# Three reorderings in a one-core encoder kernel: the opening's copies and weight split, the conv chunks in the attention, the Ln and Exp of the head norms

## The chip, the core and the metric

The kernel runs on one core of a Trainium2 chip. The core has a matrix engine (TensorE, PE in the trace), VectorE (DVE), ScalarE (ACT), GpSimd (POOL) and a queue that only starts transfers (SyncE, SP). Each engine takes its instructions in program order; between engines there are only semaphores, so an instruction that waits holds everything behind it on its engine. The metric is the time of one execution on the device, in microseconds.

## The reference, cut to what matters

```
h = x                                                          # 512 tokens x 1024
# layer 0
hn   = rms_norm(h, norm_mix[0]);  proj = hn @ w_in             # u, q, k, v
u    = silu(layer_norm(conv31(u_a * sigmoid(u_b)) + conv_b))   # 4 chunks of 128 channels
a    = softmax(s0 + bias) - lam * softmax(s1 + bias)           # 4 heads, 2 maps each
o    = rms_norm(a @ v, subln_g) * (1 - lam_init)
h   += concat([u, o]) @ w_out
# layer 1: RWKV-7 time mixing
xr, xw, xk, xv, xa, xg = [hn + hh * mu[i] for i in range(6)]
r, k, v = xr @ w_r, xk @ w_k, xv @ w_v
kk   = k * k_k;  kk = kk / max(sqrt(sum(kk^2, per head)), 1e-12)
...                                                            # two wkv7 scans, norm, gate
# after each: cross-attention into 256 memory tokens, squared-ReLU MLP (4096 hidden); at the end rms_norm
```

All is float32. The large products are made of three passes: each operand is split into a rounded high part and a low rest, and TensorE adds hi\*hi, hi\*lo and lo\*hi.

## The kernel before

Activations lie transposed: 8 chunks of 128 channels by 512 tokens. Weights come in slots of 1024 x 256 (1 MB); three raw slots `w` are filled by SyncE in turn. Each slot is split by two instructions: `Split.round` on ScalarE writes the high part (L326) and `Split.rest` on VectorE subtracts it from the raw weights (L344). Activation chunks are split in the same way, `Pair.round` (L405) and `Pair.rest` (L410). A product of 128 output channels is 24 matmuls (L357 to L359). Four PSUM banks are used in turn for numbered jobs: TensorE takes the bank of job n when the reader of job n-4 has freed it. No scheduler runs: the order on each engine is the order in which the code is written, or a list that all engines walk through.

*Opening* (`stage_in`). TensorE transposes x chunk by chunk (jobs jx+c, L651). VectorE copies chunks 0 to 3 to `h` (L799), ScalarE chunks 4 to 7 (L716), after it has summed the squares of the rows and made the roots (L710 to L712). VectorE multiplies the identity by the roots (L802), TensorE spreads them over all partitions (L655), and `Norm.start_dve` and `start_act` make the normalised chunks (L518) and their high and low parts. The first product starts when slot 0 is split and chunk 0 has its low part, and goes on chunk by chunk. `start_act` and `start_dve` already contain calls of `ws.round(act, 0)` and `ws.rest(dve, 0)`; such a call does nothing for a slot that is done.

*Differential attention* (`Differential`). All engines walk the list `order`. For i = 0 to 15, pair i is the two maps of one head and one block of queries: ("s", i, c) are its scores, TensorE's product (L972), VectorE's bias and maximum (L1026), ScalarE's exp (L1070). ("k", ...) is half a product of layer 1's memory keys, filler for TensorE (L982, copied by ScalarE in L1079). ("d", i) is the difference of the two maps on VectorE (L1034 to L1040), ("t", i) its transpose (L990, copied in L1087), "o" the product with v (L998), "n" the sum of squares for the head norm, whose Ln and Exp are ScalarE's L1105 and L1108, "m" and "M" the scaled head output and its split. ("A", c) splits conv chunk c, which is ready before the list begins: ScalarE's L405, VectorE's L410. What it makes is used by the output projection, after the list.

*Key projection of the recurrent layer* (`rin_act`, `rin_dve`). For t = 0 to 7: VectorE mixes chunk t of xv (L1900), ScalarE rounds it (L405) and copies key chunk t out of its bank (L1800), VectorE makes the low part (L410), scales the key (L1957) and squares it (L1962). TensorE sums the squares of a head (L1759), VectorE clamps the sum at 1e-24 (L1970) at step t for chunk t-2, ScalarE makes Ln and Exp, that is the reciprocal root (L1859, L1862), VectorE multiplies (L1975). Odd steps also split a weight slot. TensorE's order is k0, k1, k2, n0, k3, n1, ... k7, n5, n6, v0, n7, v1 ...; v0 needs the low part of chunk 7.

Of the kernel before, what the change touches and what calls it, by code (L numbers as in the profile page):

```python
# [21 lines left out]
ALU = mybir.AluOpType  # L22
ACT = mybir.ActivationFunctionType
# [7 lines left out]
C = D // P  # L31
# [505 lines left out]
def stage_in(k, cat):  # L537


    i = k.i  # L540
# [163 lines left out]
    def in_act(act):  # L704
# [8 lines left out]
        ws.round(act, 0)  # L713
        for c in range(4, C):
            k.wait_full(act, jx + c)
            act.activation(k.h[:, c, :], k.bank(jx + c), ACT.Copy).then_inc(k.free(jx + c), 1)  # L716
# [21 lines left out]
        for x in seq:  # L738
            kind, n = x
# [49 lines left out]
    def in_dve(dve):  # L789
# [7 lines left out]
        for c in range(4):  # L797
            k.wait_full(dve, jx + c)
            dve.tensor_copy(k.h[:, c, :], k.bank(jx + c)).then_inc(k.free(jx + c), 1)  # L799
        dve.wait_ge(s_root, 1)  # L800
        for a in range(4):
            dve.tensor_scalar(diag[:, a, :], k.ident, xst[:, 8 + a:9 + a], None, ALU.mult).then_inc(s_diag, 1)  # L802
        ws.rest(dve, 0)
# [112 lines left out]
class Differential:  # L916
# [3 lines left out]
    def __init__(self, k, cat, first):  # L920
# [17 lines left out]
        for i in range(16):  # L938
            order += [("s", i, 0), ("s", i, 1), ("k", i // 2, i % 2)]
            if i:  # L940
                order.append(("d", i - 1, 0))
            for lag, kind in ((3, "o"), (4, "n"), (5, "m"), (6, "M")):
                if i >= lag and (i - lag) % 4 == 3:
                    order.append((kind, (i - lag) // 4, 0))
            if i >= 2:
                order.append(("t", i - 2, 0))
            if i in (1, 3, 5, 7):
                order.append(("A", i // 2, 0))
# [659 lines left out]
def stage_rwkv_in(k):  # L1608
# [4 lines left out]
    with ExitStack() as cx:  # L1613
# [158 lines left out]
        def rin_act(act, lead):  # L1772
# [71 lines left out]
            for t in range(16):  # L1844
# [9 lines left out]
                if 3 <= t < 11 and t % 2:  # L1854

                    b = t - 3
                    for n in (b, b + 1):
                        k.wait_freed(act, num[("n", n)])
                        k.act(act.activation(rn[:, n % 4, :], rn[:, n % 4, :], ACT.Ln))  # L1859
                    k.act.wait(act)  # L1860
                    for n in (b, b + 1):
                        act.activation(rn[:, n % 4, :], rn[:, n % 4, :], ACT.Exp, scale=-0.5).then_inc(s_rt, 1)  # L1862
# [23 lines left out]
        def rin_dve(dve):  # L1886
# [65 lines left out]
            for t in range(16):  # L1952
# [19 lines left out]
                if 4 <= t < 12:  # L1972
                    b = t - 4
                    dve.wait_ge(s_rt, b + 1)
                    dve.tensor_tensor(kk[:, b, :], kk[:, b, :], rn[:, b % 4, :], ALU.mult).then_inc(s_kk, 1)  # L1975
# [996 lines left out]
```

## Time and profile before

| | us |
|---|---|
| three executions | 1918.66, 1923.87, 1922.09 (median 1922.09) |
| the profiled execution | 1918.66 |
| its span | 1916.8 |
| TensorE busy | 1856.4 (97%) |
| VectorE busy | 1053.4 (55%) |
| ScalarE busy | 745.4 (39%) |

Times in the rows count from the start of the span; 1.9 us of the execution lie around it. TensorE's busy time is that of pipelined instructions whose ends are modelled, so it says that the engine is fed, not that it is at its peak. Where one engine is busy nearly all the time, the places to read are its few waits and, in front of each, the queue of the engine that it waited for.

### The profile page before, as it was taken

How to read it: one execution, taken by the hardware profiler on the slowest of the kernel's cores; microseconds unless marked ns; L12 is line 12 of the kernel's file. 1: busy time of each engine (PE TensorE's matmuls, PEld its weight loads, DVE VectorE, ACT ScalarE, POOL GpSimd, SP SyncE). 2: the span in 40 equal slices, each digit the busy share in tenths (PEclk: the TensorE clock that was granted, in tenths of full speed). 3: DMA queues.
4: the chain of work that ended last, by engine and by line, in shares of the span. 5: the costliest groups of instructions: out<-in, count | busy, mean ns of one | idle time of the engine just before them, and what ended most of it. 6: DMA issues, size and time to landing. Idle time of an engine off the chain costs nothing.

```text
span 1916.8 us, 38658 instructions
## 1 busy us (share of the span) xinstructions
PE 1856.4 (97%) x17053; PEld 1527.7 (80%) x17053; DVE 1053.4 (55%) x1404; ACT 745.4 (39%) x999; POOL 174.5 (9%) x136
## 2 busy tenths in 40 slices
PE   6999999999999999999999999999999999999997
PEld 5898668778888888775779898988777788888886
DVE  4997755444432442538659787877754444324422
ACT  4534664344321332323644333443643353213322
POOL 1000002010000001210012111111220010000000
PEclk9999999999999999999999999999999999999999
DMA  6226233212233233433441111112352122332221
GB/s 214 89 87 217 76 99 132 67 62 92 88 110 98 89 99 110 162 110 127 159 141 45 50 50 50 51 47 70 125 201 85 44 88 92 106 110 87 90 88 44
DMA packets 165503, 189.41 MB, mean 99 GB/s; under 512 B 11801, under 2 KB 152646, under 8 KB 163674
## 3 DMA queue, kind: packets, MB, share of 16 engines
q1 hardware_dynamic: 162016, 174.44, 28.7%
q0 software_dynamic: 3088, 12.45, 1.6%
q8 instruction: 135, 2.21, 0.5%
q14 instruction: 30, 0.25, 0.0%
q10 hardware_dynamic: 234, 0.06, 0.0%
HBM read 161.22 MB, written 21.51 MB: 95 GB/s over the span
## 4 chain that ended last, share of the span: by engine, by line
PE 51%; DVE 4%; issue 2%; ACT 1%; DMA 1%; ACTq 0%; DVEq 0%; SPq 0%
PE ps L357 10%; PE ps L359 10%; PE ps L358 10%; PE ps L2356 7%; PE ps L2322 2%; PE ps L2369 2%; PE ps L2310 1%; PE ps L2333 1%; PE ps L1313 1%; PE ps L1743 1%; PE ps L2415 1%; PE ps L2289 1%; PE ps L2452 1%; PE ps L1294 1%; PE ps L2381 1%
## 5 line engine op out<-in xcount | busy, mean ns | idle before, releaser
L344 DVE TENSOR_TENSOR weights_split<-w,weights_split 128x2048 fp32r<-128x2048 f32 x116 | 265.6, 2290 | 235.8 <-ACT weights_split L326 231.1
L326 ACT ACTIVATE weights_split<-w 128x2048 fp32r<-128x2048 f32 x118 | 225.5, 1911 | 290.5 <-PE ps L359 270.6
L357 PE MATMUL ps<-x_hn_hi,weights_split 128*128 128x512 f32 x640 | 252.7, 395 | 0.0
L359 PE MATMUL ps<-x_hn_hi,weights_split 128*128 128x512 f32 x640 | 249.2, 389 | 0.0
L358 PE MATMUL ps<-x_hn_lo,weights_split 128*128 128x512 f32 x640 | 249.0, 389 | 0.0
L357 PE MATMUL ps<-f_hidden_hi,weights_split 128*128 128x512 f32 x512 | 199.3, 389 | 0.0
L359 PE MATMUL ps<-f_hidden_hi,weights_split 128*128 128x512 f32 x512 | 199.2, 389 | 0.0
L358 PE MATMUL ps<-f_hidden_lo,weights_split 128*128 128x512 f32 x512 | 199.2, 389 | 0.0
L1563 DVE SCALAR_TENSOR_TENSOR f_relu<-ps,x_squares 128x512 f32<-128x512 f32 x64 | 44.1, 691 | 191.1 <-PE ps L359 172.5
L358 PEld LDWEIGHTS ps<-x_hn_lo,weights_split 128*128 128x128 f32 x640 | 120.2, 188 | 26.4 <-issue 1.4
L357 PEld LDWEIGHTS ps<-x_hn_hi,weights_split 128*128 128x128 f32 x640 | 120.2, 188 | 26.0 <-issue 1.4
L359 PEld LDWEIGHTS ps<-x_hn_hi,weights_split 128*128 128x128 f32 x640 | 120.1, 188 | 25.1
L462 POOL TENSOR_TENSOR x_squares<-x_squares 128x512 f32<-128x512 f32 x36 | 50.4, 1401 | 948.8 <-ACT x_squares L454 948.1
L1447 ACT ACTIVATE f_squared<-f_relu 128x512 f32<-128x512 f32 x64 | 40.4, 631 | 200.7 <-DVE f_relu L1563 200.7
L358 PEld LDWEIGHTS ps<-f_hidden_lo,weights_split 128*128 128x128 f32 x512 | 96.1, 188 | 20.1
L359 PEld LDWEIGHTS ps<-f_hidden_hi,weights_split 128*128 128x128 f32 x512 | 96.1, 188 | 19.9
L357 PEld LDWEIGHTS ps<-f_hidden_hi,weights_split 128*128 128x128 f32 x512 | 96.1, 188 | 19.8
L357 PE MATMUL ps<-x_src_hi,weights_split 128*128 128x512 f32 x256 | 103.8, 405 | 4.6 <-DVE weights_split L344 3.3
L359 PE MATMUL ps<-x_src_hi,weights_split 128*128 128x512 f32 x256 | 99.8, 390 | 0.0
L358 PE MATMUL ps<-x_src_lo,weights_split 128*128 128x512 f32 x256 | 99.7, 390 | 0.0
L357 PE MATMUL ps<-r_mix_hi,weights_split 128*128 128x512 f32 x192 | 78.9, 411 | 4.0 <-DVE r_mix_lo L410 2.9
L2268 POOL TENSOR_TENSOR s_levels<-s_b_scores_rows,con 128x1024 f32<-128x1024 f32 x24 | 56.4, 2363 | 277.2 <-PE ps L2381 182.7
(365 smaller groups left out, 3496.7 us busy)
## 6 DMA issues: line engine op xcount, KB each, us to landing
w<-in_ffn_w_up_dram SPq DMA_DIRECT2D x32, 1024.0 KB, 5.4
w<-in_ffn_w_down_dram SPq DMA_DIRECT2D x32, 1024.0 KB, 5.0
w<-in_xattn_w_kv_dram SPq DMA_DIRECT2D x15, 1024.0 KB, 5.4
w<-in_ab_w_in_dram SPq DMA_DIRECT2D x10, 1024.0 KB, 5.1
w<-in_xattn_w_q_dram SPq DMA_DIRECT2D x8, 1024.0 KB, 5.0
w<-in_xattn_w_o_dram SPq DMA_DIRECT2D x8, 1024.0 KB, 5.0
w<-in_ab_w_out_dram SPq DMA_DIRECT2D x4, 1024.0 KB, 5.4
w<-in_rwkv_w_r_dram SPq DMA_DIRECT2D x4, 1024.0 KB, 6.5
```

The source lines that it names most:

```text
L326: act.activation(hi, raw, ACT.Copy).then_inc(k.w_hi_ready, 1)
L344: eng.tensor_tensor(lo, raw, hi.bitcast(F32), ALU.subtract).then_inc(k.w_lo_ready, 1)
L357: pe.matmul(out, lhs[0], rhs[0], start=start, stop=False)
L358: pe.matmul(out, lhs[0], rhs[1], start=False, stop=False)
L359: return pe.matmul(out, lhs[1], rhs[0], start=False, stop=stop)
L462: pool.tensor_tensor(self.acc, former, self.sq[:, c % 2, :], ALU.add).then_inc(self.s_acc, 1)
L1447: act.activation(r2[:, n % 2, :], rl[:, n % 2, :], ACT.Square).then_inc(s_r2, 1)
L1563: dve.scalar_tensor_tensor(rl[:, n % 2, :], k.bank(up[half] + n), 0.0, rs, ALU.max, ALU.mult) \
L2268: pool.tensor_tensor(lm[:, l - 1], bb[:, p % 2, :, :, 0, :], over(k.mask(f"Z{l}"), NC, 2), ALU.mult) \
L2322: m = pe.matmul(bank(kind, p, h)[HP[z], i * P:(i + 1) * P], kb[r, u, c, z, :], ar[r, b, :, c, z, :], start=True, stop=True)
L2356: m = pe.matmul(k.ps[r, 6 + h, at(c)], lhs, rhs, start=True, stop=True)
L2369: m = pe.matmul(bank(kind, p, h)[r, i * P:(i + 1) * P], xt[r, h, c, :], ra[r, c, h, :, :].rearrange("p a t -> p (a t)"), start=True, stop= ...
```

## The change

Three places are edited, with no change of what is computed. In the opening ScalarE copies chunks 4, 6 and 7 and VectorE chunk 5 (behind the diagonals), and the first weight slot is split inside `start_act` and `start_dve`, on ScalarE after the copies and on VectorE behind two normalised chunks. In the attention the four ("A", c) entries move from the ends of iterations 1, 3, 5 and 7 to iterations 1, 2, 3 and 4, ahead of the difference. In the key projection Ln and Exp are done for one chunk at each step from t=2, instead of for two chunks at each odd step from t=3, and VectorE's multiplication comes one step earlier.

```
--- before.py
+++ after.py
@@ -710,8 +710,7 @@
             k.act.link(act, act.activation(xsq[:, :], xn[:, a, :], ACT.Square, accum_out=xst[:, a:a + 1]))
         k.act.link(act, act.activation(xst[:, 4:8], xst[:, 0:4], ACT.Ln, bias=k.eps[:, 0:1], scale=1.0 / D))
         act.activation(xst[:, 8:12], xst[:, 4:8], ACT.Exp, scale=-0.5).then_inc(s_root, 1)
-        ws.round(act, 0)
-        for c in range(4, C):
+        for c in (4, 6, 7):
             k.wait_full(act, jx + c)
             act.activation(k.h[:, c, :], k.bank(jx + c), ACT.Copy).then_inc(k.free(jx + c), 1)
         nrm.start_act(act, ws)
@@ -794,13 +793,14 @@
             n = sum(r for _, r in ROWS[g])
             k.wait_full(dve, jp + g)
             dve.tensor_copy(k.par[:, g * P:g * P + n], k.bank(jp + g)[:, 0:n]).then_inc(k.free(jp + g), 1)
-        for c in range(4):
+        for c in (0, 1, 2, 3, 5):
+            if c == 5:
+                dve.wait_ge(s_root, 1)
+                for a in range(4):
+                    dve.tensor_scalar(diag[:, a, :], k.ident, xst[:, 8 + a:9 + a], None, ALU.mult) \
+                       .then_inc(s_diag, 1)
             k.wait_full(dve, jx + c)
             dve.tensor_copy(k.h[:, c, :], k.bank(jx + c)).then_inc(k.free(jx + c), 1)
-        dve.wait_ge(s_root, 1)
-        for a in range(4):
-            dve.tensor_scalar(diag[:, a, :], k.ident, xst[:, 8 + a:9 + a], None, ALU.mult).then_inc(s_diag, 1)
-        ws.rest(dve, 0)
         dve.wait_ge(s_rs, 1)
         for n in (jp + 2, *range(jx, jx + C)):
             k.wait_freed(dve, n)
@@ -937,6 +937,8 @@
         order = []
         for i in range(16):
             order += [("s", i, 0), ("s", i, 1), ("k", i // 2, i % 2)]
+            if 1 <= i <= 4:
+                order.append(("A", i - 1, 0))
             if i:
                 order.append(("d", i - 1, 0))
             for lag, kind in ((3, "o"), (4, "n"), (5, "m"), (6, "M")):
@@ -944,8 +946,6 @@
                     order.append((kind, (i - lag) // 4, 0))
             if i >= 2:
                 order.append(("t", i - 2, 0))
-            if i in (1, 3, 5, 7):
-                order.append(("A", i // 2, 0))
         order += [("d", 15, 0), ("R", "01", "01"), ("m", 2, 0), ("t", 14, 0), ("R", "01", "23"), ("M", 2, 0),
                   ("t", 15, 0), ("R", "23", "0"), ("o", 3, 0), ("R", "23", "1"), ("n", 3, 0), ("R", "01", "456"),
                   ("R", "23", "23"), ("m", 3, 0), ("M", 3, 0), ("R", "01", "7"), ("R", "23", "4567")]
@@ -1851,15 +1851,12 @@
                     ws.round(act, t // 2 + 6)
                 if t in (12, 13):
                     lead(t - 12)
-                if 3 <= t < 11 and t % 2:
-
-                    b = t - 3
-                    for n in (b, b + 1):
-                        k.wait_freed(act, num[("n", n)])
-                        k.act(act.activation(rn[:, n % 4, :], rn[:, n % 4, :], ACT.Ln))
-                    k.act.wait(act)
-                    for n in (b, b + 1):
-                        act.activation(rn[:, n % 4, :], rn[:, n % 4, :], ACT.Exp, scale=-0.5).then_inc(s_rt, 1)
+                if 2 <= t < 10:
+
+                    b = t - 2
+                    k.wait_freed(act, num[("n", b)])
+                    k.act.link(act, act.activation(rn[:, b % 4, :], rn[:, b % 4, :], ACT.Ln))
+                    act.activation(rn[:, b % 4, :], rn[:, b % 4, :], ACT.Exp, scale=-0.5).then_inc(s_rt, 1)
 
         def rin_pool(pool):
             for c in range(C):
@@ -1969,8 +1966,8 @@
                         dve.wait_ge(s_kk, b - 3)
                     dve.tensor_scalar(rn[:, b % 4, :], k.bank(num[("n", b)]), 1e-24, None, ALU.max) \
                        .then_inc(k.free(num[("n", b)]), 1)
-                if 4 <= t < 12:
-                    b = t - 4
+                if 3 <= t < 11:
+                    b = t - 3
                     dve.wait_ge(s_rt, b + 1)
                     dve.tensor_tensor(kk[:, b, :], kk[:, b, :], rn[:, b % 4, :], ALU.mult).then_inc(s_kk, 1)
         k.scan_inputs = [(s_out[b], 16 * 8) for b in range(2)] + [(s_vout[b], 16 * 4) for b in range(2)] \
```

VectorE at the start of the program. `x_roots` are the diagonals with the roots, `in_hn_full` the normalised chunks, and the rows with `weights_split` the low part of a slot.

```order
-L799 COPY h<-ps 128x512 x4
-L802 TENSOR_SCALAR x_roots<-con,x_stats 128x128 x4
-L344 TENSOR_TENSOR weights_split<-w,weights_split 128x2048
+L795 COPY par<-ps 128x117
+L795 COPY par<-ps 128x124
+L795 COPY par<-ps 128x88
+L803 COPY h<-ps 128x512 x4
+L800 TENSOR_SCALAR x_roots<-con,x_stats 128x128 x4
+L803 COPY h<-ps 128x512
 L518 SCALAR_TENSOR_TENSOR in_hn_full<-h,par,ps 128x512 x2
+L344 TENSOR_TENSOR weights_split<-w,weights_split 128x2048
 L410 TENSOR_TENSOR in_hn_lo<-in_hn_full,in_hn_hi 128x512
```

The split of the slot moved from ahead of the two normalised chunks to behind them, and a fifth copy stands ahead. The copies of `par` are those of before with other line numbers.

VectorE in the attention, from the second score of pair 1 on; before:

```order
L1026 ISA scores,softmax_stats<-ps,bias 128x512
L1026 ISA softmax_stats 128x1
L1034 RECIPROCAL softmax_stats<-softmax_stats 128x2
L1035 TENSOR_TENSOR softmax_stats<-softmax_stats,lam 128x1
L1039 TENSOR_SCALAR difference<-scores,softmax_stats 128x512
L1040 SCALAR_TENSOR_TENSOR difference<-scores,softmax_stats,difference 128x512
```

and after:

```order
L1026 ISA scores,softmax_stats<-ps,bias 128x512
L1026 ISA softmax_stats 128x1
L410 TENSOR_TENSOR x_src_lo<-cat,x_src_hi 128x512
L1034 RECIPROCAL softmax_stats<-softmax_stats 128x2
L1035 TENSOR_TENSOR softmax_stats<-softmax_stats,lam 128x1
L1039 TENSOR_SCALAR difference<-scores,softmax_stats 128x512
L1040 SCALAR_TENSOR_TENSOR difference<-scores,softmax_stats,difference 128x512
```

The low part of conv chunk 0, which before stands behind these rows, moved ahead of the difference of pair 0. Before, the next three stand behind the differences of pairs 2, 4 and 6; after, one stands ahead of each of the differences of pairs 1, 2 and 3.

ScalarE in the key projection, from the rounding of chunk 2 of xv to the step of chunk 3. `memt` holds the clamped sums.

```order
 L405 ACTIVATE r_mix_hi<-r_mixed 128x512
 L1800 ACTIVATE r_staged<-ps 128x512
+L1858 ACT_TABLE_LOAD
+L1858 ACTIVATE memt<-memt 128x512
+L1859 ACT_TABLE_LOAD
+L1859 ACTIVATE memt<-memt 128x512
 L405 ACTIVATE r_mix_hi<-r_mixed 128x512
 L1800 ACTIVATE r_staged<-ps 128x512
 L326 ACTIVATE weights_split<-w 128x2048
+L1858 ACT_TABLE_LOAD
+L1858 ACTIVATE memt<-memt 128x512
 L1859 ACT_TABLE_LOAD
```

A load, an Ln, a load and an Exp are new behind the copy of key chunk 2, where nothing stood; the odd step that follows has one Ln and one Exp where it had two and two. In this stretch the program before has 8 table loads and the changed one 16.

## Rows read from the trace of the kernel before

**Rows 1.** The page, busy time of the engines: us, share, instructions.

```profile
PE 1856.4 (97%) x17053; PEld 1527.7 (80%) x17053; DVE 1053.4 (55%) x1404; ACT 745.4 (39%) x999; POOL 174.5 (9%) x136
```

**Rows 2.** Timeline of the opening: start, duration (us), engine, line, operation, [idle before <-releaser].

```profile
14.85 1.92 ACT L326 ACTIVATE weights_split<-w 128x2048 fp32r<-128x2048 f32 x1 [0.57 <-DMA w<-in_ab_w_in_dram]
...
16.48 1.16 PE L655 MATMUL ps<-x_roots,con 128*128 128x128 f32 x8
...
16.68 2.03 ACT L716 ACTIVATE h<-ps 128x512 f32<-128x512 f32 x4
...
16.81 2.29 DVE L344 TENSOR_TENSOR weights_split<-w,weights_split 128x2048 fp32r<-128x2048 f32 x1 [0.38 <-ACT weights_split L326]
...
19.02 1.40 DVE L518 SCALAR_TENSOR_TENSOR in_hn_full<-h,par,ps 128x512 f32<-128x512 f32 x2
...
20.45 0.69 DVE L410 TENSOR_TENSOR in_hn_lo<-in_hn_full,in_hn_hi 128x512 fp32r<-128x512 f32 x1
...
21.29 0.77 PE L357 MATMUL ps<-in_hn_hi,weights_split 128*128 128x512 f32 x1 [3.65 <-DVE in_hn_lo L410]
```

**Rows 3.** Timeline in the attention, all engines, pairs 2 to 6.

```profile
202.91 0.69 DVE L410 TENSOR_TENSOR x_src_lo<-cat,x_src_hi 128x512 fp32r<-128x512 f32 x1 [0.56 <-ACT x_src_hi L405]
...
206.42 0.69 DVE L1026 CUSTOM_DVE_ANT_0 scores<-ps,bias 128x512 f32<-128x512 f32 x1
...
207.65 0.16 DVE L1034 RECIPROCAL softmax_stats<-softmax_stats 128x2 f32<-128x2 f32 x1
...
207.88 0.71 ACT L1070 ACTIVATE scores<-scores,softmax_stats 128x512 f32<-128x512 f32 x1
...
208.12 1.13 PE L972 MATMUL ps<-keys,q 64*128 64x512 f32 x4
...
208.44 0.75 DVE L1040 SCALAR_TENSOR_TENSOR difference<-scores,softmax_stats,difference 128x512 f32<-128x512 f32 x1
...
208.59 0.36 ACT L1079 ACTIVATE mem_keys<-ps 128x256 f32<-128x256 f32 x1
...
209.32 0.62 ACT L405 ACTIVATE x_src_hi<-cat 128x512 fp32r<-128x512 f32 x1
...
210.05 0.69 DVE L410 TENSOR_TENSOR x_src_lo<-cat,x_src_hi 128x512 fp32r<-128x512 f32 x1 [0.86 <-ACT x_src_hi L405]
...
211.54 1.13 PE L972 MATMUL ps<-keys,q 64*128 64x512 f32 x4
...
217.97 3.60 PE L998 MATMUL ps<-difference_t,v 128*128 128x512 f32 x8
```

**Rows 4.** Timeline in the attention, around pairs 8 to 10.

```profile
230.09 1.12 PE L972 MATMUL ps<-keys,q 64*128 64x512 f32 x2 [0.39 <-ACT difference_t L1087]
...
230.66 0.69 DVE L410 TENSOR_TENSOR x_src_lo<-cat,x_src_hi 128x512 fp32r<-128x512 f32 x1 [4.80 <-ACT x_src_hi L405]
...
237.07 1.13 PE L972 MATMUL ps<-keys,q 64*128 64x512 f32 x4
```

**Rows 5.** Timeline of the key projection, TensorE, VectorE and ScalarE.

```profile
923.40 0.62 ACT L405 ACTIVATE r_mix_hi<-r_mixed 128x512 fp32r<-128x512 f32 x1
...
925.78 0.68 DVE L1970 TENSOR_SCALAR memt<-ps 128x512 f32<-128x512 f32 x1
...
927.76 0.63 ACT L405 ACTIVATE r_mix_hi<-r_mixed 128x512 fp32r<-128x512 f32 x1 [3.26 <-DVE r_mixed L1900]
...
936.65 0.61 ACT L405 ACTIVATE r_mix_hi<-r_mixed 128x512 fp32r<-128x512 f32 x1
...
942.46 0.47 PE L357 MATMUL ps<-r_mix_hi,weights_split 128*128 128x512 f32 x1 [1.12 <-issue]
```

**Rows 6.** ScalarE's groups, 900 to 950 us: count | busy us, mean ns | idle.

```profile
L1859 ACT ACT_TABLE_LOAD x3 | 3.8, 1283 | 0.1
```

**Rows 7.** Stretches: us, busy by engine, PEclk (granted clock), DMA share, GB/s.

```profile
21.70:24.70 3.00, 3.00 (x8) 2.35 (x8) 2.93 (x6) 1.98 (x3) 0.00 (x0) 0.51 1.04 373
...
232.90:236.20 3.30, 3.30 (x8) 2.43 (x8) 3.23 (x7) 1.63 (x5) 0.00 (x0) 0.50 0.00 0
```

More of the change, by code:

```diff
@@ L712, in in_act @@
         act.activation(xst[:, 8:12], xst[:, 4:8], ACT.Exp, scale=-0.5).then_inc(s_root, 1)
-        ws.round(act, 0)
-        for c in range(4, C):
+        for c in (4, 6, 7):
             k.wait_full(act, jx + c)
@@ L796, in in_dve @@
             dve.tensor_copy(k.par[:, g * P:g * P + n], k.bank(jp + g)[:, 0:n]).then_inc(k.free(jp + g), 1)
-        for c in range(4):
+        for c in (0, 1, 2, 3, 5):
+            if c == 5:
+                dve.wait_ge(s_root, 1)
+                for a in range(4):
+                    dve.tensor_scalar(diag[:, a, :], k.ident, xst[:, 8 + a:9 + a], None, ALU.mult) \
+                       .then_inc(s_diag, 1)
             k.wait_full(dve, jx + c)
             dve.tensor_copy(k.h[:, c, :], k.bank(jx + c)).then_inc(k.free(jx + c), 1)
[L800 to L803, printed above, removed]
         dve.wait_ge(s_rs, 1)
@@ L939, in __init__ @@
             order += [("s", i, 0), ("s", i, 1), ("k", i // 2, i % 2)]
+            if 1 <= i <= 4:
+                order.append(("A", i - 1, 0))
             if i:
@@ L946, in __init__ @@
                 order.append(("t", i - 2, 0))
-            if i in (1, 3, 5, 7):
-                order.append(("A", i // 2, 0))
         order += [("d", 15, 0), ("R", "01", "01"), ("m", 2, 0), ("t", 14, 0), ("R", "01", "23"), ("M", 2, 0),
@@ L1853, in rin_act @@
                     lead(t - 12)
[L1854 to L1862, printed above, removed]
+                if 2 <= t < 10:
+                    b = t - 2
+                    k.wait_freed(act, num[("n", b)])
+                    k.act.link(act, act.activation(rn[:, b % 4, :], rn[:, b % 4, :], ACT.Ln))
+                    act.activation(rn[:, b % 4, :], rn[:, b % 4, :], ACT.Exp, scale=-0.5).then_inc(s_rt, 1)
         def rin_pool(pool):
@@ L1971, in rin_dve @@
                        .then_inc(k.free(num[("n", b)]), 1)
-                if 4 <= t < 12:
-                    b = t - 4
+                if 3 <= t < 11:
+                    b = t - 3
                     dve.wait_ge(s_rt, b + 1)
```

## The prediction

> **What bounds the kernel now.** I read the busy times first: TensorE is busy 97% of the span [rows 1]. A saving on another engine is worth nothing unless TensorE waits for it, and each wait that TensorE gains lengthens the run. So I read, for each of the three places edited, the timeline of the three engines: when a TensorE instruction waited, for whom, and how late the engine it waited for already was. The first place is the opening, where TensorE idles 3.65 us before its first weight product [rows 2]. The second is the differential attention, where TensorE is continuously fed except around 230 us [rows 3, 4]. The third is the key projection of the recurrent layer, where its one wait, 1.12 us, ends at 942.46 [rows 5]. Behind each, TensorE is the bound again and has no slack in absolute time, so a delay at one place is carried to the end.
>
> **The opening.** VectorE's order is the path. Before, it splits the first weight slot (2.29 us from 16.81) while TensorE spreads the row roots (16.48 to 17.64) and ScalarE copies x (16.68 to 18.71); the normalised chunks start at 19.02 and the first low part at 20.45 [rows 2]. After, VectorE copies chunk 5 (0.69) behind the diagonals and then waits for the root spread, which still runs from 16.48 to 17.64, as nothing ahead of the diagonals has changed. ScalarE no longer splits at 14.85; it copies three chunks, the last as soon as TensorE has transposed it (by 16.5), to about 17.1, then splits to 19.0 (1.92). VectorE: two normalised chunks from 17.7, 1.4 us; weight split from 19.1, 2.2; first low part at 21.3 instead of 20.45. What was hidden beside the root spread now stands between it and the product. From there VectorE is busy without a break to the eighth low part, so the whole start is 0.9 us late. Bounds: 0 if the split could still hide, +2.3 if all of it (the row's 2.29) is added. I take +0.9. Loading the fourth slot starts as late as that split ends, 2.3 us later, and has some 15 us before ScalarE wants it: nothing.
>
> **The attention.** Before, TensorE repeats two scores, half a key product and a transpose every 3.42 us (208.12 to 211.54) [rows 3]. VectorE takes both scores (206.42 to 207.65), then the difference of the pair before (0.79 to the start of its last instruction, 0.75 for that), and only then the low part of a conv chunk, at 210.05, for which it waits on ScalarE's rounding [rows 3]. The difference fills most of that wait. After, the low part comes first and VectorE stands still through ScalarE's latency. From the first score: the second exp starts 1.46 us later (207.88), is done 0.71 later (208.59), rounding 0.62, handover 0.11 (209.94 to 210.05): 2.90; low part 0.61; difference 1.54 and handover 0.04: 5.1 us a pair, and 0.26 more where ScalarE copies a key product in between. Four of these: the first low part stays at 202.91 [rows 3], since ScalarE's queue ahead of it is the same; with it done (0.61) and the first difference (1.58), the scores of pairs 2, 3, 4, 5 start at 205.1, 210.2, 215.55, 220.65. The fourth difference ends at 220.6, TensorE's transpose of it waits for that, then come its transpose 0.53, scores 1.06, a wait of about 1.0 for ScalarE's key copy (queued behind pair 5's exps) and half a key product 1.83: the first head product starts at 225.0 against 217.97 [rows 3], 7.05 us late. Its own 3.43 us lets VectorE catch up.
>
> What comes back: before, the fourth low part stood at pair 7, behind ScalarE's root of head 0, and VectorE waited 4.80 us for it; TensorE needed 6.98 us (230.09 to 237.07) for 3.42 us of work [rows 4], 1.5 of it because the granted clock fell to 0.50 after the waits [rows 7]. After, no low part stands there: 3.56 us return. (The 0.39 us before 230.09 waits for ScalarE's transposed copy, behind the same root, and stays.) Net 7.05 - 3.56 = +3.5. Bounds: -3.6 if the four standstills never reached TensorE; +5.1 if the clock also falls in the new waits (of 0.9 to 1.6 us each) and one stretch, worth 1.6, ends outside them. Inside them it costs nothing, since TensorE waits for VectorE anyway. I take +3.5.
>
> **The key projection.** One Ln and one Exp per chunk instead of two and two: the count of activations is the same, but each change of function brings a table load of 1.28 us [rows 6], and the order of the changed program has 16 loads here for 8. That is 10.3 us more of ScalarE. On the path is this much: before, an even step runs 4.36 us from rounding to rounding (923.40 to 927.76) and an odd one 8.89 (to 936.65) [rows 5]. An even step had no Ln. Now its first load fits into the wait for VectorE's clamp, which ends at 926.46; then Ln 0.65, load 1.29, Exp 0.54 put the next rounding at 929.0: 5.6, +1.2. An odd step waits for the clamp in both and then does one Exp less (-0.5). The first even step, t=2, has no Exp pair behind it and no kk product: 3.8 long by my estimate (4.36 less VectorE's 0.6), it becomes 5.6: +1.8. Up to the rounding of t=7: +1.8 -0.5 +1.2 -0.5 +1.2 = +3.2. TensorE's value projection needs the low part of that rounding, so it starts at 945.6 instead of 942.46 [rows 5]; the banks are freed in time and the last head norm waits under 1 us. I take +3.1. Moving VectorE's kk product one step earlier frees nothing that TensorE wants.
>
> TensorE then stands idle 3.6 us before 945.6. It stood idle 3.65 us before 21.29 and the granted clock was 0.51 in the stretch that followed, and 0.50 behind the waits at 230 to 232 us [rows 2, 4, 7]. I expect a fall to the 1.2 GHz level here too. Those two stretches last 3.0 and 3.3 us and do half the work, so it costs +1.6. Bounds for this place: 0 if the loads hide, +4.8.
>
> Two rules of the Trainium skill bear on these loads. "ScalarE: Activation LUTs", Table sets, says that one set holds both ln and exp, so that Ln followed by Exp would take one load. The rows have a load before the Ln and another before the Exp, and the order of the changed program has both too, so the trace disagrees; were the rule to hold, the place would cost nothing (second rival). The same page, What ACT_TABLE_LOAD costs, adds a drain of 1.38 us to every load; the odd step of 8.89 us [rows 5] has no room for two such drains beside its activations, so the trace disagrees. With the drain the estimate for the place would be 3 x 2 x 1.38 = 8 us more.
>
> **Sum.** 0.9 + 3.5 + 3.1 + 1.6 = +9.1 us. The profiled execution took 1918.66 us, 1.9 beyond its span of 1916.8, and would become 1927.8. It was the fastest of three; their median is 1922.09, so I forecast 1931.2.
>
> **The rivals.**
> 1. *The four low parts are hidden.* TensorE has banks ahead of VectorE, and in the trace it hardly waits in spite of holds of VectorE like the 0.86 us at 210.05 [rows 3]. Then only the gain at 230 to 237 us counts: 0.9 - 3.6 + 3.1 + 1.6 = +2.0, 1924.1, not slower. The point from which it decides is a VectorE pair of 3.42 us; the rows give 5.1, and the transpose waits for the difference of the pair before, so a buffer does not help. For it speaks only that a hold is worth less than it looks while TensorE still has key products.
> 2. *The table loads cost nothing*, because ScalarE has idle time here (3.26 us before 927.76 [rows 5]) or because the loads are shared. 0.9 + 3.5 = +4.4, 1926.5, too little to be told from none or nearly so. Against it: the idle time lies before the roundings, but the new Ln and Exp stand in front of the next one, and an odd step has no idle time at all.
> 3. *No fall of the clock at 945 us*: +7.5, 1929.6.
> 4. *The clock falls in the attention too*, at its end: +10.7, 1932.8. Waits of 0.9 to 1.6 us in every 5 resemble the 230 us place, where it fell.
> A gain over 0.3% has no mechanism here: even rivals 1 and 2 together give -2.7.
>
> **How the numbers follow.** Forecast 0.52, rival 1 0.08, rival 2 0.10, rival 3 0.14, rival 4 0.12, anything else 0.04. A measurement of this kernel tells a change from none at about 0.3%, 5.8 us. Slower: the forecast, rivals 3 and 4, less 0.03 for the spread of the medians (some 2 us): 0.75. Within 0.3%: rivals 1 and 2, that 0.03 and 0.01 of the rest: 0.22. Faster: the other 0.03 of the rest. The range 1925 to 1935 leaves out most of rival 1 below and little above; the forecast's own is 1928.5 to 1933.5.
>
> **What would show it.** Opening: VectorE's weight split behind two normalised chunks, the first TensorE product near 22.2. Attention: four holds of VectorE of 1.6 to 2 us before L410, new waits of TensorE between 205 and 223, the head product about 7 us after its old place beyond the opening's delay, and no wait of 4.80. Key projection: 16 loads, roundings 5.6 and 8.4 us apart in turn, an idle of 3.6 us before the value projection, half clock behind it. I am wrong if the head product is late by less than 4 us, or if the value projection starts at its old distance from the first key product.

## The result, and the profile after

| | before | after |
|---|---|---|
| median of four executions | 1921.24 (1918.66 to 1923.87) | 1933.93 (1930.98 to 1936.33) |
| the profiled execution | 1918.66 | 1928.18 |
| its span | 1916.8 | 1926.4 |

The changed kernel takes 1.0065 times as long as before, with a 95% interval of 1.0045 to 1.0086, that is 12.5 us more (8.6 to 16.5). The two profiled executions differ by 9.5 us; that of the changed kernel is not one of its four and shorter than all of them.

The page of the changed kernel, busy times; it answers to [rows 1]:

```profile
PE 1859.2 (97%) x17053; PEld 1529.8 (79%) x17053; DVE 1055.7 (55%) x1405; ACT 755.4 (39%) x1006; POOL 174.2 (9%) x136
```

TensorE does the same 17053 matmuls. ScalarE has 10.0 us more: the eight extra loads are 10.3. Nobody would find the 9.5 us in these shares; they are in TensorE's waits.

*Opening.* The timeline of the changed kernel, for [rows 2]:

```profile
17.10 0.69 DVE L803 COPY h<-ps 128x512 f32<-128x512 f32 x1
...
17.32 1.08 PE L655 MATMUL ps<-x_roots,con 128*128 128x128 f32 x8
...
18.06 1.91 ACT L326 ACTIVATE weights_split<-w 128x2048 fp32r<-128x2048 f32 x1
...
18.44 1.41 DVE L518 SCALAR_TENSOR_TENSOR in_hn_full<-h,par,ps 128x512 f32<-128x512 f32 x2 [0.65 <-PE ps L655]
...
20.00 2.29 DVE L344 TENSOR_TENSOR weights_split<-w,weights_split 128x2048 fp32r<-128x2048 f32 x1 [0.15 <-ACT weights_split L326]
...
22.21 0.69 DVE L410 TENSOR_TENSOR in_hn_lo<-in_hn_full,in_hn_hi 128x512 fp32r<-128x512 f32 x1
...
23.04 0.76 PE L357 MATMUL ps<-in_hn_hi,weights_split 128*128 128x512 f32 x1 [4.64 <-DVE in_hn_lo L410]
```

The split stands behind the two normalised chunks, as forecast. The product is 1.75 us later than before; 0.51 of this is the arrival of the first parameters, at which TensorE's first matmul stands in every run (11.48 here, 10.97 before). It is no part of the change.

*Attention.* The timeline from pair 2 on, for [rows 3]; the fourth low part, at 222.09, answers to the one of 4.80 us in [rows 4]:

```profile
206.32 0.69 DVE L410 TENSOR_TENSOR x_src_lo<-cat,x_src_hi 128x512 fp32r<-128x512 f32 x1 [2.02 <-ACT x_src_hi L405]
...
208.61 0.63 PE L990 MATMUL ps<-con,difference 128*128 128x128 f32 x4 [0.87 <-DVE difference L1040]
...
211.48 0.69 DVE L410 TENSOR_TENSOR x_src_lo<-cat,x_src_hi 128x512 fp32r<-128x512 f32 x1 [1.56 <-ACT x_src_hi L405]
...
213.78 0.63 PE L990 MATMUL ps<-con,difference 128*128 128x128 f32 x4 [1.37 <-DVE difference L1040]
...
216.44 1.97 PE L982 MATMUL ps<-memt,w 128*128 128x256 f32 x8 [0.79 <-ACT mem_keys L1079]
...
216.92 0.69 DVE L410 TENSOR_TENSOR x_src_lo<-cat,x_src_hi 128x512 fp32r<-128x512 f32 x1 [1.83 <-ACT x_src_hi L405]
...
222.09 0.69 DVE L410 TENSOR_TENSOR x_src_lo<-cat,x_src_hi 128x512 fp32r<-128x512 f32 x1 [1.57 <-ACT x_src_hi L405]
...
228.78 3.60 PE L998 MATMUL ps<-difference_t,v 128*128 128x512 f32 x8
```

VectorE waits 1.56 to 2.02 us before each low part. The difference comes behind it, so TensorE's transpose (L990), which takes the difference, waits as well.

*Key projection.* The changed kernel's timeline, for [rows 5], and ScalarE's groups between 900 and 950 us, for [rows 6]:

```profile
927.52 0.63 ACT L1858 ACTIVATE memt<-memt 128x512 f32<-128x512 f32 x1 [1.66 <-DVE memt L1967]
928.17 1.28 ACT L1859 ACT_TABLE_LOAD   x1
...
930.00 0.62 ACT L405 ACTIVATE r_mix_hi<-r_mixed 128x512 fp32r<-128x512 f32 x1
931.12 1.28 ACT L1858 ACT_TABLE_LOAD   x1
933.11 0.63 ACT L1858 ACTIVATE memt<-memt 128x512 f32<-128x512 f32 x1 [0.70 <-DVE memt L1967]
933.75 1.28 ACT L1859 ACT_TABLE_LOAD   x1
...
935.59 0.62 ACT L405 ACTIVATE r_mix_hi<-r_mixed 128x512 fp32r<-128x512 f32 x1
...
943.94 0.61 ACT L405 ACTIVATE r_mix_hi<-r_mixed 128x512 fp32r<-128x512 f32 x1
...
950.95 0.76 PE L357 MATMUL ps<-r_mix_hi,weights_split 128*128 128x512 f32 x1 [3.31 <-issue]
```

```profile
L1858 ACT ACT_TABLE_LOAD x5 | 6.4, 1283 | 0.1
L1859 ACT ACT_TABLE_LOAD x5 | 6.4, 1283 | 0.1
```

Roundings stand 5.59 us apart (930.00 to 935.59) and 8.35 us (935.59 to 943.94) in turn.

To read the stages apart from what lies ahead of them, each is measured between two rows of TensorE. The rows of before that close the stages:

```profile
202.34 1.99 PE L982 MATMUL ps<-memt,w 128*128 128x256 f32 x8 [0.26 <-ACT mem_keys L1079]
...
268.63 0.47 PE L357 MATMUL ps<-x_src_hi,weights_split 128*128 128x512 f32 x1 [1.93 <-DVE weights_split L344]
...
819.02 0.50 PE L357 MATMUL ps<-r_mix_hi,weights_split 128*128 128x512 f32 x1 [2.13 <-DVE r_mix_lo L410]
...
894.88 0.50 PE L357 MATMUL ps<-r_mix_hi,weights_split 128*128 128x512 f32 x1 [0.74 <-DVE r_mix_lo L410]
...
990.49 1.13 PE L2303 MATMUL ps<-s_centre,pair_in 128*128 128x128 f32 x8 [0.84 <-issue]
```

and the same instructions of the changed kernel:

```profile
205.75 1.99 PE L982 MATMUL ps<-memt,w 128*128 128x256 f32 x8 [0.27 <-ACT mem_keys L1079]
...
275.89 0.47 PE L357 MATMUL ps<-x_src_hi,weights_split 128*128 128x512 f32 x1 [1.93 <-DVE weights_split L344]
...
826.41 0.50 PE L357 MATMUL ps<-r_mix_hi,weights_split 128*128 128x512 f32 x1 [2.13 <-DVE r_mix_lo L410]
...
900.20 0.51 PE L357 MATMUL ps<-r_mix_hi,weights_split 128*128 128x512 f32 x1 [0.33 <-DVE r_mix_lo L410]
...
1000.55 1.13 PE L2300 MATMUL ps<-s_centre,pair_in 128*128 128x128 f32 x8 [0.84 <-issue]
```

The attention takes 66.29 us before and 70.14 after (+3.85), the key projection to the scans 95.61 and 100.35 (+4.74, of which 3.17 ahead of the value projection and 1.57 behind it). But the clock also did things that the change did not ask for. Windows of the changed kernel behind a wait for VectorE's gates (`glu`, L821) that ends at 45.13, in the new attention waits, behind 950.95 and behind 826.41 (columns as in [rows 7]):

```profile
46.00:49.30 3.30, 3.30 (x10) 2.61 (x9) 0.00 (x0) 0.00 (x0) 0.00 (x0) 0.56 0.03 5
207.00:228.00 21.00, 15.10 (x65) 9.21 (x64) 14.96 (x43) 10.10 (x25) 1.08 (x2) 1.00 0.20 64
951.00:954.30 3.30, 3.30 (x8) 2.62 (x9) 2.80 (x3) 2.69 (x2) 0.45 (x1) 0.50 0.98 366
826.50:829.80 3.30, 3.30 (x15) 2.83 (x16) 3.30 (x6) 0.91 (x2) 0.00 (x0) 1.00 0.00 0
```

and the first and the last of these places in the kernel before:

```profile
43.40:46.70 3.30, 3.30 (x15) 2.72 (x16) 0.00 (x0) 0.00 (x0) 0.37 (x1) 1.00 0.17 50
819.10:822.40 3.30, 3.30 (x10) 2.61 (x11) 3.30 (x6) 0.89 (x2) 0.00 (x0) 0.63 0.00 0
```

The same wait of 1.06 us (it ends at 45.13 in the changed kernel, at 43.34 in the kernel before) is followed by half clock after and by full clock before; the same wait of 2.13 us at 819 us the other way round. The first cost 1.62 us (the delay goes from 1.79 at 45.13 to 3.41 at 205.75), the second gave 2.07 back (7.39 at 826.41, 5.32 at 900.20). That stretch takes 75.42 to 76.60 us in the six traces of all those below that have a fall of the clock there, and 73.78 to 74.19 in the seven that have none. So the 9.5 us are: 0.5 arrival, 1.3 opening, 1.6 clock, 3.85 attention, 0.1 between, -2.1 clock, 3.2 and 1.6 key projection, -0.5 in and behind the scans. The last of these terms is small by luck, as the part on the prediction shows.

### The profile page after: what moved, and what is told of

It is laid out like the page before. It is cut to its first block, busy times and chain, and to the rows that moved or that the text cites. A ratio compares the mean times of both kernels' runs of the same rounds, so it can differ in the third digit from the quotient of the medians.

```text
span 1926.4 us, 38666 instructions
## 1 busy us (share of the span) xinstructions
PE 1859.2 (97%) x17053; PEld 1529.8 (79%) x17053; DVE 1055.7 (55%) x1405; ACT 755.4 (39%) x1006; POOL 174.2 (9%) x136
## 4 chain that ended last, share of the span: by engine, by line
PE 48%; DVE 5%; issue 2%; ACT 2%; DMA 0%; ACTq 0%; DVEq 0%; SPq 0%
PE ps L357 10%; PE ps L359 10%; PE ps L358 10%; PE ps L2353 7%; PE ps L2319 2%; PE ps L2366 2%; PE ps L2307 1%; PE ps L1743 1%; PE ps L2330 1%; PE ps L1313 1%; PE ps L2412 1%; PE ps L2449 1%; PE ps L1294 1%; DVE s_inverse_t L2683 1%; PE ps L2286 1%
```

## The experiments

My theory was the prediction's: three independent costs, the opening's split that is no longer hidden, the low parts ahead of the difference, and the table loads. The rivals stand with each run. All ratios are against the kernel before on the same chip, for the numbered runs from 10 to 12 executions of each and 27 to 35 of before, for the whole change from four and four; 0.1% is 1.9 us. Since one execution of this kernel can differ from the next by several us, the stage lengths of the trace carry the verdicts and the ratios check the sum.

Stage lengths of all traces, in us. *Opening*: from the first matmul (L646) to the first weight product, in brackets from the root spread (L655) to it. *Attention*: to the first head product, and to the conv product, from the 202.34 row's place. *Key*: from the 894.88 row's place to the value projection, and to the scans. *Falls*: stretches of half clock before 1900 us, each of which takes 1.66 to 1.72 us of full clock away (sums over windows of 2 us; two in a row count twice).

| kernel | opening | attention | key | falls | ratio to before |
|---|---|---|---|---|---|
| before | 10.32 (4.81) | 15.63, 66.29 | 47.58, 95.61 | 3 | |
| after | 11.56 (5.72) | 23.03, 70.14 | 50.75, 100.35 | 4 | 1.0065 |
| 1 opening | 11.35 (5.72) | 15.62, 66.34 | 47.60, 96.03 | 6 | 1.0011 |
| 2 attention | 10.17 (3.96) | 23.02, 70.14 | 47.58, 95.60 | 3 | 1.0021 |
| 3 roots | 10.49 (5.09) | 15.61, 66.33 | 50.76, 101.29 | 8 | 1.0029 |
| 4 more loads | 10.07 (4.34) | 15.61, 66.30 | 51.03, 101.92 | 7 | 1.0023 |
| 5 no loads | 10.51 (4.75) | 15.63, 66.34 | no wait, 94.37 | 4 | 0.9989 |
| 6 behind, 1234 | 10.10 (3.53) | 16.28, 63.39 | 47.59, 95.61 | 2 | 0.9989 |
| 7 behind, 1356 | 10.10 (3.70) | 15.51, 62.63 | 47.60, 95.62 | 4 | 0.9993 |
| 8 ahead, 1357 | 10.30 (4.23) | 18.52, 66.36 | 47.58, 95.61 | 5 | 1.0004 |
| 9 split kept | 10.28 (4.94) | 15.62, 66.20 | 47.60, 95.64 | 6 | 1.0008 |
| 10 after, behind | 11.90 (5.72) | 16.28, 63.39 | 50.77, 100.78 | 6 | 1.0018 |
| 11 one function | 10.23 (3.47) | 15.51, 62.62 | no wait, 94.36 | 3 | 0.9972 |

### The three edits one by one (runs 1, 2, 3)

Each run is the kernel before with one of the three pieces of the diff shown above. Run 1, the opening:

> The kernel before with the opening's edit alone. Theory (VectorE's weight split now stands between the root spread and the first product): TensorE's wait before its first weight product grows from 3.65 us to about 4.65, the first product starts 1.2 us later counted from the first row transpose, nothing is returned until the attention, and the run is longer by 1.2 us, or by 2.8 us if the granted clock also falls near 45 us, as it does with the whole change. Rival (the start is paid back from slack in the projection behind it): the wait grows, but the wait for the gates near 43 us shrinks by as much, and the run is within 0.3 us.

Run 2, the attention:

> The kernel before with the attention's edit alone: the four low parts one pair after the other, ahead of the difference. Theory (VectorE stands still through ScalarE's latency, four times): first head product 7.4 us later than before, new waits of TensorE of 0.8 to 1.4 us in every pair, the hold of 4.80 us gone, and 3.8 us of the delay left at the end of the attention and at the end of the run. Rival (the cost is only there with the shifted start of the whole change): head product late by under 3 us and a run as long as before or up to 3.5 us shorter.

Run 3, the key projection:

> The kernel before with the key projection's edit alone: one Ln and one Exp for each chunk, 16 table loads for 8, product of VectorE one step earlier. Theory (loads on ScalarE ahead of each rounding): TensorE idles over 3 us before its value projection, which starts 3.2 us later than before, the granted clock is at half for about 3 us behind it (1.6 us more), run +4.8 us. Rival A (the fall of the clock is chance, not bound to this idle time): +3.2 us. Rival B (the loads lie in idle time of ScalarE): 0 us, value projection at its old place.

Run 1 measured 1.0011 (0.9998 to 1.0023). The wait of TensorE is 4.58 us and the first product stands 1.0 us later than before. The wait for the gates is 1.06 us as before, and neither the attention nor the key projection gives anything back; the clock fell near 45 us. Run 2: 1.0021 (1.0007 to 1.0034), +4.0 us; head product +7.39, end of the attention +3.85, both to 0.01 those of the whole change, which rules out that the shifted start mattered for the attention. Run 3: 1.0029 (1.0016 to 1.0042), +5.6 us; value projection +3.18, and two stretches of half clock around it. The three ratios add up to 1.0061, the whole change has 1.0065. The intervals leave room for some us of interplay, the stage lengths do not: the attention and the key projection up to the value projection are those of the whole change to 0.01. Rival B of run 3 and both of the others are out; its rival A is not excluded by run 3 alone.

### Is it the loads? (runs 4, 5)

Run 4 keeps the pairs in their place and alternates the functions:

```
-for n in (b, b + 1): Ln(n)
-for n in (b, b + 1): Exp(n)
+for n in (b, b + 1): Ln(n); Exp(n)
```

> The kernel before with its pairs of roots in their old place, but computed as Ln, Exp, Ln, Exp instead of Ln, Ln, Exp, Exp: the same activations at the same steps, 16 table loads for 8. Theory (a load costs its 1.28 us wherever it stands ahead of a rounding on the path): each odd step 2.6 us longer, two such steps ahead of the last key rounding, value projection 5.1 us later, half clock behind the idle time: run +6.7 us, more than the edit of the change costs with as many loads. Rival (the edit costs because the root stands in every step and waits for VectorE's clamp there, not because of loads): 0 to +1 us here, as the steps and waits are the old ones.

Measured 1.0023 (1.001 to 1.0037), value projection +3.45, two falls of the clock, scans +6.31. So loads cost wherever they stand: the rival is out. The price per odd step was too high: two roundings in the timeline of run 4,

```profile
927.97 0.63 ACT L405 ACTIVATE r_mix_hi<-r_mixed 128x512 fp32r<-128x512 f32 x1 [3.25 <-DVE r_mixed L1896]
...
938.58 0.61 ACT L405 ACTIVATE r_mix_hi<-r_mixed 128x512 fp32r<-128x512 f32 x1
```

are 10.61 us apart for 8.89 [rows 5], so 1.72 more, not 2.6, and twice that is the 3.45. Before, ScalarE waited 1.01 us for VectorE's second clamp in that step; here a load and the first Exp fill that wait. The two loads are 2.57 us, so 1.56 would be left. The other 0.16 are mostly the two Exp: they took 1.06 us back to back, and take 0.66 and 0.54 with loads between. Of the 2.57 us only 0.85 were free in the end, and where a wait stands decides how much.

Run 5 is the key projection's edit with `ACT.Exp` in place of `ACT.Ln`; it leaves the logarithm out.

> The kernel before with the key projection's edit alone, its Ln replaced by a second Exp, so that the logarithm is left out and no table is loaded between the two; activations, places and waits are those of the edit. Theory (the edit costs through its table loads): the 3.2 us of the value projection's delay are gone, TensorE's wait ahead of it is 1.1 us or less as before, run 0 to -1 us against before. Rival (the edit costs because a root now waits for VectorE's clamp in every step): still 2 us or more late at the value projection.

Measured 0.9989 (0.9978 to 0.9999). TensorE has no wait before the value projection at all, and the scans come 1.24 us earlier than before. With the loads gone the same placement, with the same wait for the clamp in each step, is a gain: the loads are the whole cost of this edit.

### Which part of the move in the attention costs? (runs 6, 7, 8)

The low parts were moved in two ways: ahead of the difference, and into pairs 1 to 4. Run 6 keeps the second only, run 8 the first only; run 7 is a third order. In all three the entries at the ends of iterations 1, 3, 5 and 7 are gone, as in the change; the cut shows the new ones.

```
 if i: order.append(("d", i - 1, 0))
+if 1 <= i <= 4: order.append(("A", i - 1, 0))            # run 6
+if i in (1, 3, 5, 6): order.append(("A", ...))           # run 7
```

(in run 8 `if i in (1, 3, 5, 7)` stands ahead of the difference).

> The kernel before with the four low parts in the pairs of the change (1 to 4) but directly behind the difference instead of ahead of it. Theory (the place ahead of the difference costs, because VectorE has nothing else to do through ScalarE's latency; one per pair as such does not): holds of VectorE before these low parts under 0.7 us, first head product at most 1 us later than before, hold of 4.80 us gone, end of the attention 2.9 us earlier than before, 1.7 us more if the granted clock no longer falls behind it: run -2.9 to -4.6 us. Rival (four low parts in four pairs are too much for VectorE in any place): first head product 3 us late or more, run not shorter than before.

> The kernel before with the low parts ahead of the difference, as in the change, but in pairs 1, 3, 5 and 7 as before. Theory (the place ahead of the difference is what costs, per low part): holds of about 2 us, three of them ahead of the first head product, which comes 2.4 us late, then about 2 us instead of 4.80 at pair 7: end of the attention -0.4 us, down to -2.1 us without the fall of the clock. Rival (only the crowding into pairs 1 to 4 costs): first head product at its old place.

> The kernel before with the low parts directly behind the difference in pairs 1, 3, 5 and 6. Theory: no new wait, first head product at its old place, the hold of 4.80 us gone: run -3.4 us, or -5.1 us with the fall of the clock near 233 us gone too, and the best of the four orders. Rival (TensorE does not gain, because another wait behind ScalarE's root of head 0 ends as late as the low part did): within 1 us of before.

Run 6, VectorE's low parts and differences, and the head product:

```profile
207.38 0.75 DVE L1040 SCALAR_TENSOR_TENSOR difference<-scores,softmax_stats,difference 128x512 f32<-128x512 f32 x1
208.23 0.69 DVE L410 TENSOR_TENSOR x_src_lo<-cat,x_src_hi 128x512 fp32r<-128x512 f32 x1
...
211.98 0.69 DVE L410 TENSOR_TENSOR x_src_lo<-cat,x_src_hi 128x512 fp32r<-128x512 f32 x1 [0.38 <-ACT x_src_hi L405]
...
215.46 0.69 DVE L410 TENSOR_TENSOR x_src_lo<-cat,x_src_hi 128x512 fp32r<-128x512 f32 x1
```

The difference now lies in ScalarE's latency, and a hold is 0.38 us or none, against 1.56 to 2.02. Four low parts in four pairs cost 0.65 us at the head product, not 7.4, and the attention ends 2.90 us earlier than before, as the theory had it. The 1.7 us more that it set on the absent fall of the clock did not come, here or in run 7. Run 8 has the other half. Its low parts,

```profile
212.84 0.69 DVE L410 TENSOR_TENSOR x_src_lo<-cat,x_src_hi 128x512 fp32r<-128x512 f32 x1 [1.83 <-ACT x_src_hi L405]
...
221.18 0.69 DVE L410 TENSOR_TENSOR x_src_lo<-cat,x_src_hi 128x512 fp32r<-128x512 f32 x1 [1.83 <-ACT x_src_hi L405]
...
230.71 0.69 DVE L410 TENSOR_TENSOR x_src_lo<-cat,x_src_hi 128x512 fp32r<-128x512 f32 x1 [1.83 <-ACT x_src_hi L405]
```

are held 1.83 us although nothing is crowded, the head product is 2.89 us late (2.4 expected), and the attention as long as before (+0.07): the last low part waits 1.83 instead of 4.80 and gives back what the others cost, where I had expected a gain of 0.4 to 2.1. Place costs by itself, and crowding raises it: three low parts with free pairs between them make the head product 2.89 us late, four in a row 7.4. Run 7 ends the attention 3.66 us earlier (expected 3.4) with the head product at its old place. By time, runs 6 and 7 are 0.9989 (0.9977 to 1.0001) and 0.9993 (0.998 to 1.0006), and run 8 1.0004 (0.9993 to 1.0015): each alone cannot be told from no change, and which of 6 and 7 is the shorter only the traces say.

### The opening: the copy or the split? (run 9)

Run 9 gives VectorE chunk 5's copy as the change does, but keeps both halves of the split in their old place:

```
 ws.round(act, 0)
-for c in range(4, C):
+for c in (4, 6, 7):
...
+for c in (0, 1, 2, 3, 5):     # the diagonals ahead of 5
+    ...
 ws.rest(dve, 0)
```

> The kernel before with chunk 5's copy given to VectorE, behind the diagonals, as in the change, but with both halves of the first weight split in their old place, ahead of the root spread's end. Theory (the opening pays for the split that is no longer hidden beside the root spread, not for the copy): the first weight product 0.3 us later than before (copy 0.69 less VectorE's wait of 0.38), against 1.1 to 1.2 with the edit as it is; run +0.3 us. Rival (VectorE's extra copy is the cost): 1 us late here too.

Measured 10.28 us to the first product, as before (10.32), and 1.0008 (0.9996 to 1.0021). The copy costs nothing, the split is the cost. Which half of it was not tested apart: in the changed kernel ScalarE's half ends at 19.97, and VectorE's, which needs it, starts at 20.00. This execution has six falls of the clock, four of them in the scans, and its time (1929.48) is the longest of the run's twelve (median 1922.35).

### Do the costs add up, and can they be had away? (runs 10, 11)

Run 10 is the changed kernel with the lines for "A" and "d" swapped. Run 11 is run 7 and, in the key projection, one activation for each chunk, in the places of the change:

```
+act.activation(rn[:, b % 4, :], rn[:, b % 4, :], ACT.Abs_reciprocal_sqrt).then_inc(s_rt, 1)
```

> The whole changed kernel with one thing swapped: the four low parts directly behind the difference instead of ahead of it. Theory (the three edits add up, and the swap takes 3.9 + 2.9 us out): first head product 6.8 us earlier than in the changed kernel, run 6.8 us shorter than it, that is +3.0 us against before (1.1 opening, -2.9 attention, 3.2 key projection, 1.6 fall of the clock behind it). Rival (the attention's delay was partly due to the later start, and something else takes the time): within 3 us of the changed kernel, +9 us or more.

> The kernel before with the low parts behind the difference in pairs 1, 3, 5 and 6, and in the key projection, for each chunk, one activation of a single function (reciprocal square root) where Ln and Exp with their loads were, one step earlier. Theory (loads and the hold are the only costs, and both can be had away): attention -3.7 us as in its own run, TensorE's wait of 1.12 us before the value projection gone (-1.2 us), no fall of the clock at either place: run -4.9 us, and less than both kernels. Rival (TensorE is so full that a wait removed comes back behind it): -2 us or less.

Run 10: 1.0018 (1.0007 to 1.0029), +3.5 us; the attention is run 6's to 0.01, the key projection the change's. The swap of two entries takes 6.75 us out of the changed kernel's attention. Run 11: 0.9972 (0.996 to 0.9983), by this ratio 5.4 us less than before, where 4.9 were expected, and faster than both kernels; of the versions that compute the same it is the one that time alone tells from before as a gain. ScalarE's groups of run 11,

```profile
L1857 ACT ACTIVATE memt<-memt 128x512 f32<-128x512 f32 x8 | 5.0, 631 | 16.5 <-DVE memt L1965 16.5
L1857 ACT ACT_TABLE_LOAD x1 | 1.3, 1283 | 0.0
```

show eight activations and one load for the 16 and 16 of the change, and from 940 to 955 us TensorE is not interrupted and keeps its clock:

```profile
940.00:955.00 15.00, 15.00 (x65) 11.85 (x64) 5.98 (x8) 4.73 (x7) 0.00 (x0) 1.00 0.27 96
```

## Why the prediction was right, and where it was not

The whole: +9.1 us against the trace of before were forecast, +9.5 came; 1931.2 against a median of 1933.93, inside the range. The medians moved by 12.7 us, and the interval (8.6 to 16.5) holds the 9.1. The mechanisms were right at all three places, with one wrong reason (what comes back); that the traces meet the sum to 0.4 us is in part luck (last point). Point by point:

- **Opening, +0.9 forecast.** 1.24 in the changed kernel, 1.0 in run 1, 1.6 in run 10; against the mean of the nine traces with no edit here (10.25; run 9 not counted) the three with it (11.60) are 1.35 late. The steps behind the root spread were right: from its start to the product 5.72 us in all three, 0.91 more than before. The step that failed is "nothing ahead of the diagonals has changed", so that the spread runs from 16.48. It does not stay there: counted from the first matmul it starts at 5.34 to 6.76 us. In the old order the first product did not care (10.07 to 10.51 us whatever the spread did); in the new one it follows the spread at a fixed distance. The edit laid the path through an instruction that varies: 0.91 of the 1.24 us are the new order, 0.33 the later spread (5.84 for 5.51). The spread stands behind TensorE's 32 transposes of x. These follow one another 0.21 us apart at first and 0.11 apart later, while the granted clock reads 1.00 throughout, as in the changed kernel:

```profile
12.50:14.00 1.50, 1.50 (x9) 1.50 (x9) 0.79 (x2) 1.45 (x4) 0.00 (x0) 1.00 1.10 219
15.50:17.00 1.50, 1.50 (x15) 1.50 (x14) 1.34 (x6) 0.60 (x1) 0.00 (x0) 1.00 1.10 348
```

  The quicker pace came after 14 transposes in the kernel before, after 17 in the changed one, and after 11 (run 9) to 26 (run 11) over the 13 traces. What sets that moment stays open.
- **Attention, head product +7.05 forecast, +7.40 measured; net +3.5, measured +3.85.** The holds are those forecast and the waits too. Rival 1, that the low parts are hidden, is refuted by runs 2, 6 and 8. The mis-sized term is the lateness ahead of the head product, by 0.35, and in it the length of a pair: TensorE's transposes stand 5.17, 5.43 and 5.17 us apart (208.61, 213.78, 219.21, 224.38) where 5.1, 5.36 and 5.1 were forecast, which is 0.21; the rest comes with the first of them and was not traced further.
- **What comes back, 3.56 forecast, 3.55 measured (7.40 - 3.85).** Its size was right, and the reason I gave for 1.5 of it was wrong: it is not the fall of the clock. Run 9 has the old order and no fall there, and is as long (66.20 for 66.29 here and 66.30 to 66.34 in four more traces of the old order). Instead of running slowly TensorE waits there, as run 9's timeline shows:

```profile
237.75 1.13 PE L974 MATMUL ps<-keys,q 64*128 64x512 f32 x4 [0.85 <-ACT difference_t L1089]
...
239.42 1.99 PE L984 MATMUL ps<-memt,w 128*128 128x256 f32 x8 [0.55 <-ACT mem_keys L1081]
```

  These waits are 1.40 us. They belong to ScalarE and VectorE, whose chain sets the pace behind a hold of 4.80 us; the slow stretch only covered them. It fits that run 8, free of the fall, gained nothing from that.
- **Clock in the attention (rival 4).** The granted clock is 1.00 through all of 207 to 228 us: refuted here, though TensorE waited six times in it, up to 1.37 us. Run 2 has a fall at 274 us, right behind the attention, where the wait of 1.93 us is in the kernel before too.
- **Key projection, +3.1 forecast, +3.17 measured, +3.18 and +3.19 in runs 3 and 10.** Roundings 5.59 and 8.35 apart for 5.6 and 8.4; TensorE's idle time was 3.31 us for 3.6. Run 5 shows that it is the loads, run 4 that of 2.57 us of two of them only 0.85 hide where ScalarE waits anyway; together they refute rival 2. On the rule of the Trainium skill in "ScalarE: Activation LUTs", Table sets, that one set holds ln and exp: the trace disagrees, the changed kernel loads a table before each of the eight Ln and each of the eight Exp. On the drain that the Trainium skill adds in What ACT_TABLE_LOAD costs of the same page: in run 3 an Exp starts at 926.95, 0.02 us after the end of the load of 925.65, so no 1.38 us stand between, and in the rows of the changed kernel above the load of 928.17 starts 0.02 us after the end of the Ln before it: the trace disagrees.
- **Fall of the clock at the value projection, +1.6 forecast, +1.57 measured.** Rival 3 is refuted as far as these traces go: the four kernels with an idle time of 2.1 us and more there (2.51 and 2.11 in run 4, 3.31 in the others) all show a fall, the nine with 1.42 us or less show none. At 819 us the same wait of 2.13 us brought a fall in six of the 13 traces only, so four of four stays a small sample. Behind the start of the value projection run 10 pays 1.98 us, and runs 3 and 4, with two in a row, 2.50 and 2.86, so +1.6 was the lower end.
- **Not forecast.** A fall near 45 us, +1.6, and one fewer at 819 us, -2.1. They nearly cancel in the trace, and neither belongs to an edit: of the 13 traces 7 have the fall near 45 us, five of them with the split in its old place, and run 10, with the changed opening, has none. In the sum of the two profiled executions this was luck of 0.5 us. The larger luck lies in the scans and what follows them, which no run edits. From the first product of the scans (L2303) to TensorE's last matmul it is 916.1 us before and 915.6 after, but 914.5 to 927.6 over the 13 traces, and it goes with the falls in it: 916.1 and 916.2 with none, 914.5 to 918.4 with one (five traces; the changed kernel has its one near 1236 us), 919.7 twice with two, 920.5 to 924.4 with three, 927.6 with four. So the stage lengths carry the argument, and the 9.5 us do not prove the sum of 9.1.

Left open: what makes the clock fall behind one wait and not behind an equal one, and with it the length of the scans in a given execution.

## What to carry to other kernels

An instruction that waits for another engine's latency should stand behind work that its own engine has ready; moving it one place ahead of that work turned a gain of 2.9 us into a loss of 3.85 here. Count an activation with the table load that its neighbour forces on it (1.28 us), and look first for one function that does the work of two. When a stage ends in a wait and a slow stretch, do not book both: the chain of the other engines may fill the time either way.

## What the runs showed of the hardware that was not expected

Half clock comes in portions: in the 13 traces a stretch takes 1.66 to 1.72 us of full clock away, or twice this. There are two to eight such portions before 1900 us, at places that change from one execution to the next behind equal waits. Where TensorE has no slack one costs its 1.6 to 2.1 us, where it would wait anyway nothing. In the scans and behind them, the same program in all 13 traces, the length runs from 914.5 us with one portion to 927.6 with four. Executions of the kernel before ran from 1914.85 to 1927.96 us, as wide a spread; the executions without a trace do not show their portions. ScalarE's reciprocal square root took 631 ns for 128x512, like Ln or Exp, and one load for eight uses.
